# Recurrence of a two-block transformer kernel: second head's corner masks on GpSimd's keys, its corner copies on ScalarE, and the decay exponentials between the inverse's levels

## The reference, cut to what matters

```
def step(S, inp):
    w_t, k_t, v_t, kk_t, a_t = inp[:5]
    sa = jnp.einsum('bhvk,bhk->bhv', S, -kk_t)
    S = (S * w_t[:, :, None, :] + sa[..., None] * (kk_t * a_t)[:, :, None, :]
         + v_t[..., None] * k_t[:, :, None, :])
    y = jnp.einsum('bhvk,bhk->bhv', S, inp[5]) if len(inp) == 6 else None
    return S, y
```

## Time and the profile before

| what | value |
| --- | --- |
| median of 3 runs | 3481.15 us |
| lowest and highest | 3478.91 and 3484.01 us |
| profiled execution, its own time as its page gives it, the span from first to last instruction | 3482.6 us |
| TensorE busy | 3297.8 us (95%) |
| VectorE busy | 1566.6 us (45%) |
| ScalarE busy | 1024.9 us (29%) |
| GpSimd busy | 1101.6 us (32%) |
| chain that ended last, TensorE's share | 82% |

### The profile page before, as it was taken

One profiled execution on the slowest core, in us unless ns is written; L12 is line 12 of the kernel. 1 busy time (PEld: TensorE's weight loads), 2 busy tenths in 40 slices (PEclk: granted clock), 3 DMA queues, 4 the chain that ended last, 5 costly groups with the idle time before them and its releaser, 6 DMA issues.

```text
span 3482.6 us, 75230 instructions
## 1 busy us (share of the span) xinstructions
PE 3297.8 (95%) x32575; PEld 2451.7 (70%) x32575; DVE 1566.6 (45%) x2774; ACT 1024.9 (29%) x1744; POOL 1101.6 (32%) x765
## 2 busy tenths in 40 slices
PE   8987899999989999999999989999999999989998
PEld 3445678633347776788888855558888888768886
DVE  3255742511128876243344350226666666543233
ACT  3043242311124366231111131333333333242221
POOL 0062142123323001332233120045555555334441
PEclk9998999999989999999999999999999999999999
DMA  4311054389971100311121124330000000022221
GB/s 161 124 49 79 30 212 170 145 328 360 369 289 52 37 2 1 122 61 61 49 73 62 66 76 181 145 112 8 16 16 16 16 16 11 4 97 97 85 109 49
DMA packets 63094, 344.27 MB, mean 99 GB/s; under 512 B 17290, under 2 KB 17306, under 8 KB 26288
## 3 DMA queue, kind: packets, MB, share of 16 engines
q1 hardware_dynamic: 40320, 291.52, 21.7%
q0 software_dynamic: 18736, 36.94, 3.1%
q10 hardware_dynamic: 3712, 11.01, 0.8%
HBM read 377.68 MB, written 28.84 MB: 117 GB/s over the span
## 4 chain that ended last, share of the span: by engine, by line
PE 82%; DVE 8%; DMA 4%; ACT 3%; issue 2%; POOL 1%; DVEq 0%; ACTq 0%; POOLq 0%
PE psum L486 23%; PE psum L498 10%; PE psum L499 10%; PE psum L500 10%; PE psum L2592 4%; PE psum L3575 3%; PE psum L2619 2%; PE psum L871 2%; PE psum L845 2%; DMA ring<-in_wall,arena 2%; PE psum L516 2%; PE psum L3558 1%; PE psum L3862 1%; DVE arena L3281 1%; PE psum L512 1%
## 5 line engine op out<-in xcount | busy, mean ns | idle before, releaser
L486 PE MATMUL psum<-arena 64*64 64x64 f32 (+5 forms) x13456 | 633.7, 236 | 35.9 <-issue 14.5
L486 PEld LDWEIGHTS psum<-arena 64*64 64x64 f32 (+2 forms) x13456 | 525.0, 139 | 104.4 <-issue 65.5
L546 POOL TENSOR_TENSOR ring_low<-ring,slab_high 128x2048 fp32r<-128x2048 f32 x66 | 304.0, 4620 | 606.2 <-ACT slab_high L539 606.2
L498 PE MATMUL psum<-h_high,slab_high 128*128 128x512 f32 (+1 forms) x1008 | 357.5, 355 | 2.6 <-POOL ring_low L546 2.6
L499 PE MATMUL psum<-h_low,slab_high 128*128 128x512 f32 (+1 forms) x1008 | 357.3, 354 | 0.0
L500 PE MATMUL psum<-h_high,ring_low 128*128 128x512 f32 (+1 forms) x1008 | 357.0, 354 | 0.0
L486 PE MATMUL psum<-arena,ring 128*128 128x512 f32 (+3 forms) x832 | 315.2, 539 | 1.8 <-DVEq L1493 1.0
L486 PEld LDWEIGHTS psum<-arena,ring 128*128 128x128 f32 (+2 forms) x832 | 156.1, 189 | 157.4 <-issue 148.4
L1154 DVE TENSOR_TENSOR arena<-arena,psum 128x512 f32<-128x512 f32 x66 | 39.5, 598 | 471.4 <-PE psum L500 467.2
L498 PEld LDWEIGHTS psum<-h_high,slab_high 128*128 128x128 f32 x1008 | 191.1, 190 | 29.5 <-POOL ring_low L546 2.8
L499 PEld LDWEIGHTS psum<-h_low,slab_high 128*128 128x128 f32 x1008 | 191.1, 190 | 26.3
(11 more groups left out here) (552 smaller groups left out, 6063.6 us busy)
## 6 DMA issues: line engine op xcount, KB each, us to landing
ring<-in_wall SPq DMA_DIRECT2D x179, 1024.0 KB, 5.5
arena<-in_wall SPq DMA_DIRECT2D x96, 1024.0 KB, 12.1
spill<-arena ACTq DMA_DIRECT2D x8, 768.0 KB, 11.4
arena<-spill POOLq DMA_DIRECT2D x16, 384.0 KB, 3.5
filters<-arena POOLq DMA_DIRECT2D x2, 2048.0 KB, 6.6
arena<-filters POOLq DMA_DIRECT2D x2, 2048.0 KB, 14.7
arena<-moe_out POOLq DMA_DIRECT2D x8, 512.0 KB, 7.2
arena<-in_tabs POOLq DMA_DIRECT2D x2, 1536.0 KB, 11.5
```

The lines of the kernel that those rows point to most:

```text
L486: last = L.eng.matmul(out, a, b, start=(i == 0), stop=(i == len(pairs) - 1))
L498: L.eng.matmul(out, a_hi, b_hi, start=(i == 0), stop=False)
L546: L.eng.tensor_tensor(m.low[:, n % SLOTS, :], m.ring[:, n % SLOTS, :], m.high_of(n).bitcast(F32), ALU.subtract).then_inc(m.sem("slab_split ...
```

## The change

GpSimd gets a new function. Once a unit, behind the start of the inverse, it multiplies the second head's `B.nt` by the mask of each of the five levels and writes five tiles of 128x384 into the space of the context's residual, which is free by then (all but its first 128 columns, which are already in use). The mask is that of the other side (7 + 2i - d in place of 6 + 2i + d), as it now stands on the keys and not on their product. The second head's corner product reads these keys, so that its result is already masked. VectorE's mask of that head goes away, and ScalarE copies the result from PSUM to `B.x`. The first head stays as it was.

The four exponentials are dealt out. The first (with the wait for `decay_sum`) goes behind the copy of the second level when the next unit is even, and of the fourth when it is odd; the other three go behind the copy of the third or fifth level.

```diff
+        ctx_place = m.xc[:, :, :].rearrange("p a b -> p (a b)")
+        self.corner_keys = [ctx_place[:, P + TT * CH * i:P + TT * CH * (i + 1)] for i in range(5)]
...
-def decay_exp_scalar(L, m, B, u):
+def decay_exp_scalar(L, m, B, u, parts=(0, 1, 2, 3)):
     e = L.eng
-    L.eng.wait_ge(m.sem("decay_sum"), L.nth("decay_sum"))
-    e.activation(u.rh, B.cm[:, 0:T], ACT.Exp, scale=DECAY_SCALE).then_inc(L.step, 1)
...
+    if parts[0] == 0:
+        L.eng.wait_ge(m.sem("decay_sum"), L.nth("decay_sum"))
+        e.activation(u.rh, B.cm[:, 0:T], ACT.Exp, scale=DECAY_SCALE).then_inc(L.step, 1)
+        L.eng.wait_ge(L.step, L.next_step())
+    if parts[-1] == 3:
+        e.activation(B.cm, B.cm, ACT.Exp, scale=-DECAY_SCALE).then_inc(L.step, 1)
...
+def corner_keys_pool(L, m, B, u):
+
+    nt = of_head(B.nt, 1)
+    for i, keys in enumerate(B.corner_keys):
+        mask = B.masks[:, (7 + 2 * i - u.d) * CH:(8 + 2 * i - u.d) * CH]
+        L.eng.tensor_tensor(tiled(keys), nt, over(mask, TT), ALU.mult).then_inc(m.sem("corner_keys"), 1)
...
@@ unit_tensor
-            corner.append(squares_tensor(L, hh, lambda *at: [(square(B.nt, *at), square(B.ti, *at))]))
+            if hh == 0:
+                corner.append(squares_tensor(L, hh, lambda *at: [(square(B.nt, *at), square(B.ti, *at))]))
+            else:
+                L.eng.wait_ge(m.sem("corner_keys"), L.nth("corner_keys"))
+                keys = B.corner_keys[LEVELS.index(lv)]
+                corner.append(squares_tensor(L, hh, lambda hh, tt, p: [(square(keys, 0, tt, p), square(B.ti, hh, tt, p))]))
...
@@ unit_scalar
     for lv in LEVELS:
-        for _ in range(2):
-            L.next_bank()
+        L.next_bank()
+        ps = L.next_bank()
+        L.eng.wait_ge(L.bank_full, L.fill)
+        copy(of_head(B.x, 1), tiled(ps[:, :TT * CH]), 1.0)
...
-    if after is not None:
-        decay_exp_scalar(L, m, B, after)
+        if after is not None and lv == LEVELS[1 if after.d == 0 else 3]:
+            decay_exp_scalar(L, m, B, after, (0,))
+        if after is not None and lv == LEVELS[2 if after.d == 0 else 4]:
+            decay_exp_scalar(L, m, B, after, (1, 2, 3))
...
@@ unit_vector
     def corner(hh, i):
-        read(of_head(B.x, hh), masked(6 + 2 * i + d))
+        if hh == 0:
+            read(of_head(B.x, hh), masked(6 + 2 * i + d))
+        else:
+            L.next_bank()
...
@@ recurrence_pool
         inverse_start_pool(L, m, B, Unit(B, n))
+        corner_keys_pool(L, m, B, Unit(B, n))
```

More of the change, by code:

```diff
@@ L3784, in decay_sum_pool @@
     L.nth("decay_sum")
-def decay_exp_scalar(L, m, B, u):
+def decay_exp_scalar(L, m, B, u, parts=(0, 1, 2, 3)):
     e = L.eng
-    L.eng.wait_ge(m.sem("decay_sum"), L.nth("decay_sum"))
-    e.activation(u.rh, B.cm[:, 0:T], ACT.Exp, scale=DECAY_SCALE).then_inc(L.step, 1)
[L3791 to L3797, removed]
+    if parts[0] == 0:
[4 more added lines that the diff above has]
+        e.activation(B.cm, B.cm, ACT.Exp, scale=-DECAY_SCALE).then_inc(L.step, 1)
+        L.eng.wait_ge(L.step, L.next_step())
+        e.activation(u.al, u.al, ACT.Exp, scale=DECAY_SCALE).then_inc(L.step, 1)
+        L.eng.wait_ge(L.step, L.next_step())
+        e.activation(u.ecol, u.ecol, ACT.Exp, scale=DECAY_SCALE).then_inc(m.sem("decay_exp"), 1)
+        L.eng.wait_ge(m.sem("decay_exp"), L.nth("decay_exp"))
 def keys_pool(L, m, B, u):
```

## The result

The changed kernel takes 3486.93 us (median of 20 runs, 3480.19 to 3497.53), the kernel before 3481.2 (20 runs, 3476.52 to 3485.26). The ratio is 1.0015, with a 95% interval of 1.0009 to 1.0022: slower by 5.7 us, where 2.1 us less were forecast. The profiled execution's span is 3489.8 us, 7.2 more than that of before; it is of a run that took 3491.84 us, one of the slower ones.

What follows compares the result with a forecast made beforehand. TensorE, busy for 691 of the recurrence's 704 us, was taken as the bound. Levels win 6.5 us, scans cost 1.8 and unit 0 2.6: 2.1 us gained, forecast 3479.1 us, range 3470.5 to 3490.

Steps and rivals of the forecast that it cites:

- The ceiling: Levels' waits for the second head's mask: at most 10.8 us to win over all units.
- the replay: Levels replayed with ScalarE's copy: 2.98 and 3.18 us in turn, 0.53 us won per odd unit, 0.27 per even; 6.5 altogether.
- GpSimd's products and what they hide under: Five products per unit, 4.8 to 5.3 us, fit GpSimd's idle time without making `decay_sum` late: cost nothing.
- The scans: VectorE's scans and GpSimd's products wait on each other: 0.25 us per even unit, 1.8 altogether; another 1.8 in unit 0.
- The alternation that L1918 suggested: VectorE waits for one GpSimd operation at most, then GpSimd waits; scans and products in turn cost unit 0 1.8 us.
- The exponentials: ScalarE's exponentials, same work but later: hidden in odd and even units, so no cost.
- TensorE's clock: Lower level for 3.41 us in the odd unit; the only cost added was 0.8 us in unit 0.
- The sum: Whole kernel: 6.5 - 1.8 - 2.6 = 2.1 us gained.
- the rival: Scan waits lower TensorE's clock in even units too: 1.7 us by 7 units, 12 us slower, 3491; chance 0.17.
- two gaps of about 0.4 us each: In the odd unit, TensorE's gaps said to precede the lower clock, after a run of two-column products.

Runs made afterwards that it cites:

- e7: Changed kernel with the four exponentials put back behind the levels in ScalarE's program: 3534.54 us, 1.0157 of the kernel before.
- e4: Kernel before with the 12 two-column head-sum products at the odd units' start computed 64 columns wide: 3469.0 us, 0.9966 of before.
- e8: Repeat of e4 (kernel before with wide head sums), on one chip with e10 and e11: 3471.19 us, 0.9971 of before.
- e10: Repeat of e5 (changed kernel with wide head sums), beside e8: 3470.55 us, 0.9968 of before.
- e2: Changed kernel with GpSimd's later products moved behind the scans or the next unit's decay sum: 3484.89 us, 1.0009 of before.
- e1: Kernel before with GpSimd's five masked products per unit and TensorE's wait for them added, their results unread: 3488.06 us, 1.0017 of before.
- e3: Changed kernel run once more, unaltered: 3485.41 us, 1.0012 of the kernel before.
- e5: Changed kernel with the wide head sums of e4: 3470.29 us, 0.9963 of the kernel before.
- e6: Changed kernel with wide head sums and the late products of e2: 3469.26 us, 0.9959 of the kernel before.
- e11: Repeat of e6 (changed kernel, wide head sums, late products), beside e8: 3466.61 us, 0.9958 of before.

## Why the prediction was wrong

*The ceiling and the replay* held for the even units: 0.28 us against 0.27. For an odd unit 0.53 was forecast (0.46 to 0.66). Its levels are 0.71 shorter in five units of eight, more than the replay allowed, since corner 1 waits less than the replay's 0.15 us and the levels don't take turns between 2.98 and 3.18 us; and 0.2 is given back right behind them, where the replay had ended. That 0.5 is left is luck: two misses that cancel. Where it goes back:

```profile
2584.77 1.61 PE L3590 MATMUL psum<-arena 64*64 64x64 f32 x48
2586.41 0.80 PE L486 MATMUL psum<-arena 64*64 64x64 f32 x20
```

48 products in a row, issued in 1.40 us, would have let the first solve start at 2586.22; it starts at 2586.41, though correction 0 is just over in time, at 2586.16. In all 16 units of the changed kernel the first solve starts 0.25 us behind that correction, where corner 1 starts 0.06 behind its own; why is open. In the even units it was there before, too, where these blocks ran without a gap; in the odd ones the wait for mask 1 had covered it.

*GpSimd's products and what they hide under* held: 4.81 to 5.23 us, no wait of TensorE for them, `decay_sum` not late by their length.

*The scans* held: 0.31 us for most even units against 0.25, with scans of 0.88 and 1.02 us; 1.82 us in unit 0 against 1.8. The alternation that L1918 suggested is what unit 0 shows, three scans in 3.6 us and five products in 5.96. The Trainium skill ("SBUF — State Buffer", "Who interferes with whom") says that a VectorE instruction with two SBUF inputs contends with a GpSimd one that reads SBUF, without naming the scan. The scan is such an instruction, and these rows agree: 0.88 and 1.02 us beside the products, 0.69 alone.

*The exponentials* held for their place, and e7 shows what they cost elsewhere.

*TensorE's clock* is the step that failed. The sum has no term for the odd units' low clock: it took its length as unchanged, without a reason, and the rival looked for a new fall in the even units alone. None came there. What happened is that in the odd units, where the clock already fell, it fell earlier and stayed low longer in five of seven, twice as long in four of them. The earlier trace rows show one unit with 3.4 us; the trace before has three with 6.8, so the length varied already. The falls are worth 12.4 (e4) and 11.5 us (e8) to the kernel before, and with the narrow products gone none is left in the odd units. With them the change costs 5.7 us by the medians (7.8 in the recurrence); without them it wins 0.6 (costs 1.4). So the missing term is 6.3 us by the medians and 6.4 in the recurrence.

What is left is a smaller miss: -2.1 forecast, -0.6 (medians) or +1.4 (recurrence) measured between e8 and e10. By the parts, unit 0 costs 1.4 us more than forecast, with its low clock (6.8 us in e10, 0 in e8); the odd units win 0.8 less, the even units' waits cost 0.7 more, and 0.7 lies in small pieces.

The prediction also misread what stands before the fall. It names "two gaps of about 0.4 us each" in the odd unit. The trace before has one of 0.25 and one of 0.20 us, and 0.11 us between them:

```profile
2547.17 0.27 PE L3862 MATMUL psum<-arena 64*64 64x64 f32 x2 [0.25 <-DVE arena L3873]
...
2554.80 0.33 PE L3862 MATMUL psum<-arena 64*64 64x64 f32 x4 [0.20 <-DVE arena L3882]
```

The even unit starts with the same 0.25 and 0.11 and keeps its clock, so only 0.20 us of waiting sets them apart, besides the narrow products.

What stays open: what makes the low stretch longer. e2 (shorter levels, no waits) has 54.6 us of low clock, e1 (waits, levels as before) 41.0, the two profiles of the changed kernel 61.4 and 54.6, before 37.5. That points to the shorter levels, with one or two profiles each. But the traces show something closer to it: how long the low stretch lasts goes with where in the unit it begins. In the five profiles with narrow sums (before, changed, e1, e2, e3), a fall that comes 7.7 to 8.4 us behind the odd unit's start lasts 3.4 us, one at 5.4 to 7.5 lasts 6.8, and the four earlier ones last 10.2 or 13.7. The earliest of the changed kernel, in unit 3, comes at 3.2 us, before that unit's narrow products have begun, behind this pause of TensorE:

```profile
2462.93 0.33 PE L486 MATMUL psum<-arena 64*64 64x64 f32 x5 [0.96 <-issue]
```

No other profile has a pause as long in these stretches. That fall the narrow products can't have brought by themselves.

So a change that only shifts a unit against the falls might do the same as shorter levels. No run here separates the two: one that lengthens a unit by a microsecond and leaves the levels alone would.

## What to carry to other kernels

Before costing a change of a microsecond a stage, look where the granted clock is at its lower level; if there is such a place in the loop, its length isn't a constant of the kernel, and it can take more than the change gives. Widening narrow products, which cost no time, took out 11.5 to 12.4 us here with an edit in two places, more than the whole rearrangement. When work moves to GpSimd, lay it so that no VectorE operation with two inputs in SBUF on the critical path runs beside it; and when an engine that ran ahead begins to wait in every step, deal out what stood behind.

## What was not expected of the hardware

In unit 9 the time from the second level's copy to the third's is 0.27 us longer than in unit 5; the chain lists the time as ScalarE's issue:

```profile
2755.90 0.02 ACTq L4030
2755.92 0.33 issue
2756.24 0.50 ACT arena L4001
```

It is what makes that unit's levels 13.8 us in place of 13.55. The six other traces with the dealt exponentials (e2, e3, e5, e6, e10, e11) have 13.8 in unit 9 too, and e7, with the exponentials behind the levels, has 13.5 in every odd unit. So the delay comes with dealing them out; how, is open. Of the narrow products, the surprise is that 12 products of 2 and of 64 columns take 1.50 and 1.55 us, and that at the odd units' start the clock falls with the first kind only.
